# Implied waits dropped, one reciprocal moved and a sign kept negative in two attentions

## The reference

```
# first block: 8 heads of 64, no mask
s = einsum('bqkgd,bskd->bkgqs', qi, k) * scale
p = softmax(s, axis=-1)
o = einsum('bkgqs,bskd->bqkgd', p, v)

# second block: 16 heads of 64, causal, with a decay per head
s = einsum('bhqd,bhkd->bhqk', q, k[..., :q1]) * scale
s = s + fcum[..., q0:q1, None] - fcum[..., None, :q1]
s = where(kpos <= qpos, s, -inf)
o = einsum('bhqk,bhkd->bhqd', softmax(s, axis=-1), v[..., :q1])
```

## Time and profile before

| | us |
|---|---|
| median of 3 runs | 2623.56 (2619.59 to 2625.0) |
| span of the profiled execution | 2619.9 |
| PE busy | 2539.2 (97%) |
| DVE busy | 1587.0 (61%) |
| ACT busy | 1233.5 (47%) |
| POOL busy | 1132.0 (43%) |
| first attention, by the maximum's instructions (L2573) | 256.9 to 457.6 |
| second attention, by the maximum's instructions (L2568) | 1853.3 to 2336.0 |

### The profile page before, as it was taken

How to read it: one execution, slowest core, us unless ns; L and a number is a source line. 1 busy time by engine, 2 the same in 40 slices (tenths; PEclk the granted TensorE clock), 3 DMA queues, 4 the chain that set the end, 5 groups by cost and what they waited for, 6 DMA issues and landing times.

```text
span 2619.9 us, 33861 instructions
## 1 busy us (share of the span) xinstructions
PE 2539.2 (97%) x12946; PEld 2112.9 (81%) x12946; DVE 1587.0 (61%) x2413; ACT 1233.5 (47%) x1858; POOL 1132.0 (43%) x754
## 2 busy tenths in 40 slices
PE   5999999999999999999999999999999999999998
PEld 3788788777888888878788888888888888888886
DVE  7654889578555566575833366666666666655333
ACT  4343888445444443333533345543656656652132
POOL 0222434437878774444487334233322222235233
PEclk8999999999999999999999999999999999999999
DMA  6134000432222126553233322222111111157342
GB/s 271 65 121 129 1 1 1 142 101 83 94 77 92 73 100 226 192 177 109 107 113 121 121 73 89 81 69 93 57 53 53 49 49 57 60 206 279 146 185 97
DMA packets 84465, 275.89 MB, mean 105 GB/s; under 512 B 9392, under 2 KB 9520, under 8 KB 84304
## 3 DMA queue, kind: packets, MB, share of 16 engines
q1 hardware_dynamic: 84304, 273.71, 29.8%
HBM read 219.54 MB, written 54.13 MB: 104 GB/s over the span
## 4 chain that ended last, share of the span: by engine, by line
PE 81%; DVE 10%; ACT 5%; issue 2%; POOL 1%; DMA 0%; DVEq 0%; SPq 0%; ACTq 0%; POOLq 0%
PE ps L609 12%; PE ps L611 11%; PE ps L610 11%; PE ps L977 7%; PE ps L978 7%; PE ps L979 7%; PE ps L848 5%; PE ps L829 4%; PE ps L1034 3%; PE ps L1036 3%; PE ps L1035 3%; DVE wf L3047 2%; PE ps L805 2%; PE ps L806 2%; DVE st L2573 1%
## 5 line engine op out<-in xcount | busy, mean ns | idle before, releaser
L3374 POOL TENSOR_TENSOR hl<-raw,hl 128x1024 fp32r<-128x1024 f32 x161 | 403.6, 2509 | 929.9 <-ACT hl L1393 929.9
L609 PE MATMUL ps<-ht,hl 128*128 128x512 f32 x1552 | 633.7, 408 | 10.5 <-DVE ht L2444 5.4
L611 PE MATMUL ps<-ht,hl 128*128 128x512 f32 x1552 | 608.4, 392 | 0.0
L610 PE MATMUL ps<-ht,hl 128*128 128x512 f32 x1552 | 608.2, 392 | 0.0
L609 PEld LDWEIGHTS ps<-ht,hl 128*128 128x128 f32 x1552 | 293.6, 189 | 71.3 <-issue 6.2
L611 PEld LDWEIGHTS ps<-ht,hl 128*128 128x128 f32 x1552 | 293.0, 189 | 63.7
L610 PEld LDWEIGHTS ps<-ht,hl 128*128 128x128 f32 x1552 | 294.0, 189 | 54.2 <-issue 1.7
L3451 POOL TENSOR_SCALAR wf<-wf,st 128x1024 f32<-128x1024 f32 (+2 forms) x192 | 167.9, 874 | 343.1 <-DVE st L2581 287.4
L1393 ACT ACTIVATE hl<-raw 128x1024 fp32r<-128x1024 f32 x163 | 171.4, 1053 | 182.2 <-PE ps L1036 66.5
L2384 DVE TENSOR_TENSOR ps<-ps,wf 128x512 f32<-128x512 f32 x116 | 80.8, 697 | 152.1 <-PE ps L979 151.9
L829 PEld LDWEIGHTS ps<-cst,wf 128*128 128x128 f32 x1088 | 126.6, 141 | 56.2 <-issue 34.4
(11 more groups left out here) (287 smaller groups left out, 5298.5 us busy)
## 6 DMA issues: line engine op xcount, KB each, us to landing
raw<-in_wst SPq DMA_DIRECT2D x243, 512.0 KB, 4.0
wf<-scratch_rows SPq DMA_DIRECT2D x32, 512.0 KB, 5.0
scratch_g<-wf SPq DMA_DIRECT2D x22, 512.0 KB, 2.6
wf<-scratch_g SPq DMA_DIRECT2D x44, 256.0 KB, 4.4
wf<-in_xT SPq DMA_DIRECT2D x16, 512.0 KB, 8.0
htf<-in_wst SPq DMA_DIRECT2D x16, 512.0 KB, 15.4
scratch_ys<-wr SPq DMA_DIRECT2D x16, 512.0 KB, 4.8
ht<-scratch_ys SPq DMA_DIRECT2D x32, 256.0 KB, 6.0
```

The lines of the kernel that those rows point to most:

```text
L609: self.op.matmul(out, wh, xh[:, c], start=(j == 0), stop=False)
L610: self.op.matmul(out, wh, xl[:, c], start=False, stop=False)
L611: t = self.op.matmul(out, wl, xh[:, c], start=False, stop=(j == kt - 1))
L3374: self.op.tensor_tensor(K.hl[:, u * 2048 + 1024:u * 2048 + 2048], K.raw[:, i % 3 * 1024:(i % 3 + 1) * 1024], hi.bitcast(F32), ALU.subtract ...
```

## The change

It has four parts.

1. Waits that another wait already implies are dropped on PE, ACT, DVE and POOL: for instance, POOL no longer awaits the exponential before it awaits the reciprocal of its sum, and PE no longer awaits `phi` where it awaits `plo`.
2. In the first attention, DVE does the reciprocal one pass later: in pass `s`, behind the maximum of tile `s + 2`, the reciprocal of tile `s + 1`, and then the subtractions of tile `s`.
3. In the first attention, PE awaits `weighed` of tile `g - 2` ahead of the last of the four score products of tile `g`.
4. In the second attention the queries (times -0.125 instead of 0.125) and the mask are negated. DVE's fused instruction adds the decay to the negated scores and keeps the minimum, which is the negated maximum; the multiplication by -1 falls away, and the exponential gets scale -1.

```diff
 scores (PE):
+            if c.stop == nk and weighed is not None:
+                self.wait_ge(*K.at("weighed", A, weighed))
             t = self.op.matmul(out, qs, K.wrr(kl)[:, c], start=False, stop=not diag)
...
-        free = (("top", A, g),) if causal else (("top", A, g), ("exp", A, g))
+        free = (("top", A, g),) if causal else (("exp", A, g),)
 turn (PE):
-            self.emptied[4 + bk] = (("phi", A, g, half), ("plo", A, g, half))
+            self.emptied[4 + bk] = (("plo", A, g, half),)
 attend1 (PE), scores of tile s:
-                         ("stackhi2", "q", 4, 1)))
+                         ("stackhi2", "q", 4, 1)), s - 2 if s >= 2 else None)
 start (ACT):
-        self.op.activation(K.maskr[:, :], K.c_mask, ACT.Copy, scale=-NEG,
-                           bias=NEG).then_inc(*self.done("maskr"))
+        self.op.activation(K.maskr[:, :], K.c_mask, ACT.Copy, scale=NEG,
+                           bias=-NEG).then_inc(*self.done("maskr"))
 soft (ACT):
-        if causal:
-            self.wait_ge(*K.at("minus", A, g))
-        else:
-            self.wait_ge(*K.at("scores", A, g))
+        if not causal:
             if g >= 4:
-                for half in (0, 1):
-                    self.wait_ge(*K.at("turn", A, g - 4, half))
+                self.wait_ge(*K.at("turn", A, g - 4, 1))
...
-        if g >= 16:
-            self.wait_ge(*K.at("weighed", A, g - 16))
-        self.op.activation(pw, pw if causal else K.ps[g % 2][:, 0:nk], ACT.Exp, bias=m, scale=1.0,
-                           accum_out=den).then_inc(*self.done("exp", A, g))
+        self.op.activation(pw, pw if causal else K.ps[g % 2][:, 0:nk], ACT.Exp, bias=m,
+                           scale=-1.0 if causal else 1.0, accum_out=den).then_inc(*self.done("exp", A, g))
 attend2 (ACT and DVE), at four places:
-        self.stack_high(w(23), (0, 1), ("q2", 0), 0.125)
+        self.stack_high(w(23), (0, 1), ("q2", 0), -0.125)
 top (DVE), second attention:
-            self.op.tensor_tensor_reduce(pw, ps, K.w(20 + h % 2)[:, 0:nk], 1.0, -3.0e38,
-                                         ALU.subtract, ALU.max, m).then_inc(*self.done("top", A, g))
-            self.wait_ge(*K.at("top", A, g))
-            self.op.tensor_scalar(m, m, -1.0, None, ALU.mult).then_inc(*self.done("minus", A, g))
+            self.op.tensor_tensor_reduce(pw, ps, K.w(20 + h % 2)[:, 0:nk], 1.0, 3.0e38,
+                                         ALU.add, ALU.min, m).then_inc(*self.done("top", A, g))
 turn (DVE):
-            self.wait_ge(*K.at("turn", A, g, half))
             self.wait_ge(*K.at("phi", A, g, half))
 attend1 (DVE):
                 self.top(1, s + 2, (s + 2) // 8, (s + 2) % 8, 0, False)
+            if 0 <= s + 1 < 64:
+                self.soft(1, s + 1)
...
                 self.turn(1, s, s % 8, pt1(K, (s // 2) % 2), False)
-            if s + 2 < 64:
-                self.soft(1, s + 2)
 weigh (POOL):
-        self.wait_ge(*K.at("exp", A, g))
         self.wait_ge(*K.at("rd", A, g))
```

More of the change, by code:

```diff
@@ L791, in project1, with scores @@
         self.mark("stage", "project1")
-    def scores(self, A, g, h, qt, q, kh, kl, causal, ready):
+    def scores(self, A, g, h, qt, q, kh, kl, causal, ready, weighed=None):
         K = self.K
@@ L839, in back @@
             for half in range((((qt if gg == g else qt - 1) + 1 if causal else 8) + 3) // 4):
-                self.wait_ge(*K.at("phi", A, gg, half))
                 self.wait_ge(*K.at("plo", A, gg, half))
@@ L2211, in attend2 @@
                     self.wait_ge(*K.at("qraw", p + 1, 1))
-                    self.stack_high(w(23), (0, 1), ("q2", p + 1), 0.125)
+                    self.stack_high(w(23), (0, 1), ("q2", p + 1), -0.125)
                 if p == 7 and s == LAST_FILL:
@@ L2560, in top @@
         self.wait_ge(*K.at("scores", A, g))
-        if g >= 16:
-            self.wait_ge(*K.at("exp", A, g - 16))
         if causal:
@@ L3235, in attend2 @@
         self.stack_low(K.ps[0], (2, 4), (3, 5), ("k", 0), 1.0, True)
-        self.stack_low(w(23), (0, 1), (0, 1), ("q2", 0), 0.125)
+        self.stack_low(w(23), (0, 1), (0, 1), ("q2", 0), -0.125)
         late = steps(0)
@@ L3263, in attend2 @@
                 if s == 15 and p < 7:
-                    self.stack_low(w(23), (0, 1), (0, 1), ("q2", p + 1), 0.125)
+                    self.stack_low(w(23), (0, 1), (0, 1), ("q2", p + 1), -0.125)
                 if p == 7 and s == LAST_FILL:
```

## The result

| | before | changed |
|---|---|---|
| median of 4 runs, us | 2624.28 (2619.59 to 2625.09) | 2640.95 (2638.57 to 2643.74) |
| span of the profiled execution | 2619.9 | 2639.1 |
| first attention, first to last maximum | 200.7 | 220.9 |
| from there to the second attention's first maximum | 1395.7 | 1396.4 |
| second attention, first to last maximum | 482.7 | 480.6 |

The changed kernel is slower: the ratio of its time to that before is 1.0069, 95% interval 1.0054 to 1.0083. The table splits the span by the start of the maximum's instructions. All of the loss lies in the first attention (+20.2 us), and the second gives back 2.1 us. Each of the two other parts moves by 0.7 us or less.

The account below looks back on a forecast made before the run. PE was taken as the bound. From 2619.9 us, +23.7 (first attention's longer period), +0.3 (its start) and -1.5 (second attention) gave 2642.4; 3.7 from span to median made 2646 us, range 2632 to 2658.

Parts of the forecast that it names:

- The ring and its leg: First attention: each maximum hangs on the previous tile's through reciprocal and weighing, 3.15 us a step; period 6.87 against 6.08.
- the leg with `back`: First attention, even tile's last score product to odd tile's: 3.72 us of PE work covers 3.15, so the wait is free.
- The dropped wait on POOL: POOL's weighing in the first attention no longer awaits the exponential: taken as 0, at best -5 us.
- PE's dropped waits: Waits on PE already implied by a later-met wait: dropping them was taken as worth 0.
- The product behind a wait: First attention, PE's product starting after a stop: up to 0.08 us more each, +2.4 us in all, left to the range.
- POOL to PE: Step from the end of a POOL instruction to PE's start, taken as 0.13 us.
- The remark on part 3: PE's new wait in the first attention is not the main culprit; without it PE would wait one place later, at the transposes.
- The offset: The median before lies 3.7 us above its profile's span; with it the forecast of 2642.4 became 2646 us.
- A: First attention: a weighing releases PE 0.3 us before its recorded end, period 6.57 us, kernel 2637 us; chance 8%.
- B: First attention: PE's gaps lower the clock in each period, +51 us on top, 2697 us; chance 5%.
- C: First attention: weighing is quick enough not to matter, PE loses its stops, -12 us, kernel 2610 us; chance 5%.
- D: Nothing happens: second attention's gain cancels the first's loss, or misread slack absorbs DVE's move; 2623 us, chance 3%.

Follow-up runs that it names:

- kernels with the reciprocal in its place: Changed kernel with the first attention's reciprocal at its old place, with PE's wait for the weighing at the scores (2617.34 us) or without it (2621.48 us).
- part 4 alone: Kernel before plus only the sign change in the second attention: 2621.67 us, ratio 0.9995.
- parts 1 and 3 alone: Kernel before plus the dropped waits and PE's wait for the weighing at the scores; reciprocal and signs as before: 2620.14 us, ratio 0.999.
- part 2 alone: Kernel before plus only the later reciprocal in the first attention, all waits and signs as before: 2640.8 us, ratio 1.0069.
- no part 3: Changed kernel without PE's wait for the weighing ahead of the last score product: 2635.63 us, ratio 1.0047 to the kernel before.
- parts 1 and 4: Kernel before plus the dropped waits and the sign change, reciprocal at its old place: 2621.48 us, and 2619.86 us when run again.
- parts 1, 3 and 4: Changed kernel with the reciprocal back at its old place in the first attention: 2617.34 us, and 2620.12 us when run again.

## Why the prediction was right

- *The ring and its leg.* Right in place, kind and size. Forecast: a period of 6.87 us, one gap of about 1.3 us ahead of the fourth score product. Measured: 6.81 and 1.03. Steps: 0.43 (0.44 forecast), 1.15 (1.12), 0.24 (0.33), 1.12 (1.13), 0.06 (0.13), in all 3.00 instead of 3.15; the leg with `back` is 456.64 - 452.83 = 3.81 instead of 3.72. The last product of that leg stands in this row:

```profile
456.64 0.39 PE L808 MATMUL ps<-wr 128*128 128x512 f32 x1
```

- *The sizes that were off.* The dropped wait on POOL, put at 0 with a bound of 5 us, was worth 0.07 to 0.09 us in each ring, that is 2 to 3 us. PE's dropped waits, put at 0 too, are worth the 0.07 us of a period in the kernels with the reciprocal in its place. The product behind a wait, left to the range at 0.08, costs 0.11 (0.34 instead of 0.23 us to the transposes). POOL to PE was read from an FFN row at 0.13 and is 0.06; in that row PE awaits two engines, which the last section takes up. Together the period grew by 0.73, not 0.79. And 20.2 us of growth is that of 27.7 such periods, not 30. Counted from the second maximum, the first two grow by 0.53 and 0.26 us only. Around 345 us, where ACT loads its function table for other work and back, periods were long already before, and one even shrinks, from 7.35 to 6.85; two later ones grow by 0.4. ACT there, in the changed kernel:

```profile
344.73 1.28 ACT L1431 ACT_TABLE_LOAD   x1
...
348.59 1.28 ACT L1640 ACT_TABLE_LOAD   x1
```

- *The remark on part 3* ("not the main culprit") holds for the larger share only: 8.0 of 22.0 us are part 3's, and only while the reciprocal is late.
- *Part 4.* -1.5 forecast; the second attention is 2.1 us shorter, of which 1.2 appear with part 4 alone and 0.7 with parts 1 and 3 alone. (With part 2 alone, whose second attention is that of before, it came out 0.5 us longer, so the 0.7 is hardly told from scatter.)
- *The offset.* The profile after is at 2639.1, the sum said 2642.4: 3.3 us off. The rest of the miss of 5 us is the 3.7 us from span to median, which was 1.9 us after. A run's own time lies only 1.8 us above its span (2640.87 and 2639.1). By that the profiled execution of before took some 2621.7 us (an estimate), 1.9 under its median: it was one of the faster ones.
- *The rivals.* A (a shorter ring by 0.3 us) was half true, by 0.15 us and for another reason. B did not happen: gaps of over 1 us in each 6.8 us for 200 us left the clock at 1.00, and the one fall, behind the gap at 265 us, is there in both kernels. What the Trainium skill says of gaps repeated in a loop (TensorE: Matmul & The Clock Gate, section "HAM oscillation") does not show for gaps of this length here. C and D fall with the measured slowdown.

On the two pages of the Trainium skill about waits: what VectorE: DVE Perf Modes (section "The DRAIN you can't avoid") says, that a semaphore after each instruction costs nothing extra, does not extend to a second awaited engine. A subtraction on DVE starts 0.70 us behind ACT's first high part where it awaits ACT and PE (part 2 alone, 428.82 - 428.12), and 0.63 us where it awaits ACT alone (no part 3, 429.36 - 428.73):

```profile
428.12 1.09 ACT L1660 ACTIVATE ht<-ps 128x512 fp32r<-128x512 f32 x2 [0.84 <-PE ps L829]
428.82 0.69 DVE L2596 TENSOR_TENSOR ht<-ps,ht 128x512 fp32r<-128x512 f32 x1 [0.35 <-ACT ht L1660]
```
```profile
428.73 1.09 ACT L1655 ACTIVATE ht<-ps 128x512 fp32r<-128x512 f32 x2 [0.77 <-PE ps L831]
429.36 0.69 DVE L2584 TENSOR_TENSOR ht<-ps,ht 128x512 fp32r<-128x512 f32 x1 [0.21 <-ACT ht L1655]
```

Perfetto Trace Analysis of the Trainium skill (section "Identifying Dependency Chains") has it that an instruction which awaits several engines may get extra semaphore instructions ahead of it. The traces agree; the last section has the counts.

## What to carry to other kernels

In a pipeline written by hand, list for each pass the loop that an edit closes from one tile to the next, add its steps from the trace, and set it against each leg of the bounding engine's own work, not against the mean. A tiny instruction moved behind a long one delays all who wait for it by the long one; whether that costs is decided by the leg with the least cover, and the same move may be free on the next tile. To fill a wait of 0.2 us on an engine that is not the bound, 1.8 us of slack were spent elsewhere.

## What was not expected of the hardware

- A wait that was met long ago can cost 0.07 to 0.09 us. A POOL instruction that awaits one engine instead of two starts 0.24 to 0.26 instead of 0.32 to 0.34 us behind the start of a 0.16 us DVE instruction; the subtraction above gains 0.07 us. Of the engines that an instruction awaits, the trace gives all but the last to separate instructions on the same queue. From 256 to 460 us the kernel before has these (PEldq is PE's queue), and the kernel with parts 1 and 3 has 2, 3 and 1 in their place:

```profile
L374 PEldq EVENT_SEMAPHORE  x125: 51/51/51, 259.5 to 459.6; - x125
L374 POOLq EVENT_SEMAPHORE  x66: 17/17/17, 259.7 to 456.8; - x66
L374 DVEq EVENT_SEMAPHORE  x172: 21/21/21, 265.9 to 459.3; - x172
```

  Which engine comes last decides whether it costs. The separate instruction ahead of the first transposes holds DVE's semaphore, the transposes themselves hold POOL's. Where DVE comes last they start 0.135 us behind its signal, the update of its semaphore in the trace (31 times before, 32 times with parts 1 and 4), against 0.045 us where they await DVE alone (parts 1, 3 and 4). Where POOL comes last they start 0.044 us behind its signal, though three engines are awaited with part 2 alone (17 times) and two without part 3 (31 times). No run changes the order of the waits, so this is read from the traces only.
- In the odd heads the period is 0.12 to 0.13 us longer in every kernel, the one before too (6.20 against 6.08). There DVE's L2604 (L2592) reads and writes the upper 64 partitions of `htf`, and the instruction behind the next maximum then starts 1.25 to 1.26 us behind it instead of 1.15. In the changed kernel, in an odd head (451.41 - 450.26 is that of an even one):

```profile
303.39 0.43 DVE L2592 TENSOR_TENSOR htf<-ps,htf 64x256 f32<-64x256 f32 x1 [0.71 <-ACT htf L1663]
...
303.91 1.23 DVE L2564 TENSOR_REDUCE st<-ps 128x1 f32<-128x1024 f32 x1
...
305.17 0.16 DVE L2570 RECIPROCAL st<-st 128x1 f32<-128x1 f32 x1
```

  The reciprocal starts only when the maximum has ended (303.91 + 1.23 = 305.14). The Trainium skill gives such a rule, as a model, in VectorE: DVE Perf Modes, section "Two Vector instructions with no wait between them": an instruction whose input starts in another quadrant of partitions than what was last read from that memory is held until the ones ahead of it have finished. The rows agree with it; it was not tested by itself. Sixteen periods at 0.12 us are 2 us of this kernel.
- Two executions of the same kernel can reach the first attention 5 us apart (259.5 and 254.2 us in the two profiles of parts 1 and 4). Against that, an effect of 4 us needs its stage time beside the median.
